# Index scores of two heads side by side, and accumulators emptied every 2.5 counting rounds instead of 2.8

## The reference, cut to what matters

```python
rel = jax.nn.relu(jnp.einsum('bqhd,bsd->bqhs', qi, k_idx))
score = jnp.einsum('bqh,bqhs->bqs', wi, rel).astype(jnp.float32)
score = jnp.where(key_pos[None, None, :] <= tq[None, :, None], score, -jnp.inf)
_, idx = lax.top_k(score, k_sel)
```

## Time and profile before

| | us |
|---|---|
| median of 3 runs | 4440.09 |
| lowest and highest | 4439.41, 4443.5 |
| the profiled execution | 4443.01 |
| its span in the trace | 4441.0 |
| TensorE busy (share of the span) | 3583.1 (81%) |
| VectorE busy | 2140.6 (48%) |
| GpSimd busy | 1159.3 (26%) |
| ScalarE busy | 1107.1 (25%) |
| mean granted clock of TensorE | 0.896 |

### The profile page before, as it was taken

One profiled execution on the slowest core, in us unless ns is written; L12 is line 12 of the kernel. 1 busy time (PEld: TensorE's weight loads), 2 busy tenths in 40 slices (PEclk: granted clock), 3 DMA queues, 4 the chain that ended last, 5 costly groups with the idle time before them and its releaser, 6 DMA issues. The chain is left out here.

```text
span 4441.0 us, 49671 instructions
## 1 busy us (share of the span) xinstructions
PE 3583.1 (81%) x18450; PEld 2762.6 (62%) x18450; DVE 2140.6 (48%) x3709; ACT 1107.1 (25%) x1965; POOL 1159.3 (26%) x654
## 2 busy tenths in 40 slices
PE   6787677657767677779999996689989778997978
PEld 4356555446666566568888785466756567665657
DVE  3579388774444424335555556503335450333552
ACT  2344133321112111110000001213335320333540
POOL 2013122212222344345444341231110233211112
PEclk7779889868888789889999998799989989998999
DMA  2001000000001111112221220210000121100011
GB/s 96 24 19 38 15 3 3 1 7 1 0 0 66 38 48 33 37 49 93 83 80 66 90 90 10 77 39 23 17 13 3 67 72 44 29 20 7 9 58 62
DMA packets 227900, 169.74 MB, mean 38 GB/s; under 512 B 42232, under 2 KB 214976, under 8 KB 226976
## 3 DMA queue, kind: packets, MB, share of 16 engines
q1 hardware_dynamic: 225152, 166.83, 12.0%
q10 hardware_dynamic: 2592, 0.81, 0.1%
HBM read 150.69 MB, written 16.92 MB: 38 GB/s over the span
## 5 line engine op out<-in xcount | busy, mean ns | idle before, releaser
L1434 DVE TENSOR_TENSOR I-12785S<-I-12785S,c_causal 128x256 f32<-128x256 f32 x64 | 27.7, 432 | 462.9 <-PE I-12785S L1372 462.9
L747 DVE TENSOR_TENSOR I-9738act_f<-I-9737act_g,I-9744p_u 128x1024 f32<-128x1024 f32 x22 | 26.9, 1222 | 321.9 <-PE I-9744p_u L259 167.3
L864 DVE SCALAR_TENSOR_TENSOR y_T<-y_T 128x1024 f32<-128x1024 f32 x48 | 131.9, 2786 | 0.0
L737 ACT ACTIVATE I-9737act_g<-I-9743p_g 128x1024 f32<-128x1024 f32 x22 | 22.6, 1029 | 419.5 <-PE I-9743p_g L259 419.5
L255 PE MATMUL I-9743p_g<-hf_hi,I-9719w_hi 128*128 128x512 f32 x352 | 109.5, 392 | 5.2 <-POOL hf_lo L473 5.2
L763 DVE TENSOR_TENSOR x_T<-x_T,I-9746p_d 128x512 f32<-128x512 f32 x176 | 112.5, 678 | 0.7 <-PE I-9746p_d L728 0.6
L763 DVE TENSOR_TENSOR x_T<-x_T,I-9745p_d 128x512 f32<-128x512 f32 x176 | 112.4, 677 | 0.4 <-PE I-9745p_d L728 0.4
L257 PE MATMUL I-9743p_g<-hf_lo,I-9719w_hi 128*128 128x512 f32 x352 | 109.0, 391 | 0.0
L259 PE MATMUL I-9743p_g<-hf_hi,I-9721w_lo 128*128 128x512 f32 x352 | 108.8, 390 | 0.0
L255 PE MATMUL I-9744p_u<-hf_hi,I-9720w_hi 128*128 128x512 f32 x352 | 108.4, 389 | 0.0
L257 PE MATMUL I-9744p_u<-hf_lo,I-9720w_hi 128*128 128x512 f32 x352 | 108.4, 389 | 0.0
(11 more groups left out here) (1035 smaller groups left out, 10457.1 us busy)
## 6 DMA issues: line engine op xcount, KB each, us to landing
y_T<-in_w_ada SPq DMA_DIRECT2D x48, 512.0 KB, 6.8
saved_x<-x_T SPq DMA_DIRECT2D x3, 4096.0 KB, 13.7
x_T<-saved_x SPq DMA_DIRECT2D x3, 4096.0 KB, 15.6
I-9717w_raw<-in_w_gate SPq DMA_DIRECT2D x22, 512.0 KB, 3.8
I-9718w_raw<-in_w_up SPq DMA_DIRECT2D x22, 512.0 KB, 4.1
I-12773w_raw<-in_w_in SPq DMA_DIRECT2D x16, 512.0 KB, 3.9
I-12774w_raw<-in_w_in SPq DMA_DIRECT2D x14, 512.0 KB, 3.9
I-9731d_raw<-in_w_down SPq DMA_DIRECT2D x11, 512.0 KB, 4.8
```

Of the source, the lines that this page charges most:

```text
L747: nc.vector.tensor_tensor(act_f[:, :], act_g[:, :], flat(p_u), ALU.mult).then_inc(product, 1)
L864: self.nc.vector.scalar_tensor_tensor(out=self.raw[s], in0=self.raw[s], scalar=1.0, in1=self.c_row, op0=ALU.mult, op1=ALU.mult, accum_out= ...
L1434: self.nc.vector.tensor_tensor(diag, diag, tiled(self.mask, 2), ALU.add).then_inc(self.masked, 1)
```

## The change

The units become (pair, tile, part of at most 512 columns), 40 of them: ten parts per pair, six of 512 columns, two of 384, one of 256 and one of 128. Each unit has both heads: two matmuls, on partitions 0 to 63 and 64 to 127, into the two banks of one score buffer; one Relu over both banks; and two weighings. VectorE does the weighing of a unit's second head one unit late, so that the first head of unit u comes, then the second head of unit u - 1. `project(2)` and `project(3)` stand in the middle of pairs 0 and 1. The conditions for writing a score or Relu buffer again are as before, counted anew. In counting, the rule for the rounds after which a `keep` runs is changed from `(r + 1) * 5 >= (done + 2) * 14` to `(r + 1) * 4 >= done * 10 + 8`.

```diff
-    units = [(n, h, t) for n in range(PAIRS) for h in range(2) for t in tiles]
+    parts = [(t, at, min((t + 1) * P - at, BANK)) for t in tiles for at in range(0, (t + 1) * P, BANK)]
+    units = [(n, t, at, w) for n in range(PAIRS) for t, at, w in parts]
...
-        relu = [v_T[:, s, :] for s in range(4)]
+        relu = [v_T[:, s, :].rearrange("p (h n) -> p h n", h=2) for s in range(4)]
...
-                for u, (n, h, t) in enumerate(units):
-                    if h == 1 and t == tiles[0] and n + 2 < PAIRS:
+                for u, (n, t, at, w) in enumerate(units):
+                    if u % len(parts) == len(parts) // 2 and n + 2 < PAIRS:
                         project(n + 2)
                     pe.wait_ge(q_ready, n + 1)
                     wait(pe, relu_done, u - 1)
-                    rows = slice(h * IDX_DIM, (h + 1) * IDX_DIM)
-                    score_columns(nc, S[u % 2], qi[n][rows, t * P:(t + 1) * P], key_T[rows, :], (t + 1) * P).then_inc(scores_ready, 1)
+                    for h in range(2):
+                        rows = slice(h * IDX_DIM, (h + 1) * IDX_DIM)
+                        last = nc.tensor.matmul(S[u % 2][:, h, 0:w], qi[n][rows, t * P:(t + 1) * P], key_T[rows, at:at + w], start=True, stop=True)
+                        last.then_inc(scores_ready, 1)
...
-                for u, (n, h, t) in enumerate(units):
-                    if h == 0 and t == tiles[0]:
+                for u, (n, t, at, w) in enumerate(units):
+                    if u % len(parts) == 0:
                         for m in ((0, 1) if n == 0 else (n + 1,) if n + 1 < PAIRS else ()):
                             act.wait_ge(q_used, m + 1)
                             nc.scalar.activation(qi[m], flat(acc[m % 2]), ACT.Copy).then_inc(q_ready, 1)
-                    w = (t + 1) * P
-                    act.wait_ge(scores_ready, u + 1)
-                    wait(act, weighed, u - 3)
-                    nc.scalar.activation(relu[u % 4][:, 0:w], flat(S[u % 2])[:, 0:w], ACT.Relu).then_inc(relu_done, 1)
-                act.wait_ge(weighed, len(units))
+                    act.wait_ge(scores_ready, 2 * (u + 1))
+                    wait(act, weighed, 2 * u - 5)
+                    nc.scalar.activation(relu[u % 4][:, :, 0:w], S[u % 2][:, :, 0:w], ACT.Relu).then_inc(relu_done, 1)
+                act.wait_ge(weighed, 2 * len(units))
...
-                    if done < NB and (r + 1) * 5 >= (done + 2) * 14:
+                    if done < NB and (r + 1) * 4 >= done * 10 + 8:
                         keep(done)
                         done += 1
...
-                for u, (n, h, t) in enumerate(units):
-                    w = (t + 1) * P
-                    dve.wait_ge(relu_done, u + 1)
-                    wait(dve, weighed, u - NS + 1)
-                    v.scalar_tensor_tensor(out=scores(t), in0=relu[u % 4][:, 0:w], scalar=head_w[:, t, 2 * n + h:2 * n + h + 1], in1=scores(t),
+
+                def weigh(u, h, after):
+                    n, t, at, w = units[u]
+                    into = scores(t)[:, at:at + w]
+                    wait(dve, weighed, after)
+                    v.scalar_tensor_tensor(out=into, in0=relu[u % 4][:, h, 0:w], scalar=head_w[:, t, 2 * n + h:2 * n + h + 1], in1=into,
                                            op0=ALU.mult, op1=ALU.add).then_inc(weighed, 1)
-                dve.wait_ge(weighed, len(units))
+
+                for u in range(len(units) + 1):
+                    if u < len(units):
+                        dve.wait_ge(relu_done, u + 1)
+                        weigh(u, 0, 2 * (u - len(parts)) + 3)
+                    if u > 0:
+                        weigh(u - 1, 1, max(1, 2 * (u - 1)))
+                dve.wait_ge(weighed, 2 * len(units))
```

## The result

The changed kernel takes 4382.5 us (median of 4 runs, 4382.0 to 4387.64) against 4441.8 for the kernel before (4 runs beside it, 4439.41 to 4451.33): 59.3 us less, a ratio of 0.9865 with a 95% interval of 0.9848 to 0.9882. The forecast was 4387, range 4375 to 4404. The profiled execution took 4382.19 us, its span is 4380.2.

What follows compares the result with a forecast made beforehand. Taken as bounds in turn: TensorE in scoring, VectorE in counting, TensorE in the tail. Scoring -35.6, extra splits +3.9 and tail -21.8 gave -53.5 us, from the median 4440.1 to 4387 us, range 4375 to 4404.

Steps and rivals of the forecast that it cites:

- Heads side by side: Scoring: two heads' matmuls overlap on TensorE, a pair costing 7.0 us, or 14.1 at 1.2 GHz, instead of 28.7.
- rival (e): Scoring: heads don't overlap, TensorE stays at 28.7 us a pair and only the tail gains, 4422 us; chance 0.04.
- 52.4 us of weighings: Scoring: VectorE's weighings for 8 heads, 6.56 us per head, priced from undisturbed durations in the earlier trace.
- Rival (d): Scoring: every weighing pays a hand-off of up to 0.2 us, its partner only just written, 4403 us; chance 0.04.
- project(2) 1.4 and project(3) 0: Scoring: VectorE's uncovered wait for project(2) is 1.4 us; project(3) finds a longer lead and costs nothing.
- The clock, 1.0: Scoring: an allowance of 1.0 us in all for falls of TensorE's granted clock.
- rival (b): The clock stays low through scoring and project(3) is uncovered, +8.5 us, 4395 us; chance 0.10.
- The split in scoring, 2.0: Scoring: POOL's weight-block split beside one 512-column weighing adds 2.0 us, 2.772 instead of 0.751.
- Two more splits at 1.95: Before ScalarE's last Sign: 15 splits instead of 13, at 1.95 us each, add 3.9 us.
- The rule of the shared port: VectorE beside GpSimd splits: full blocking would cost 4.3 us a split, 7.0 us more in sum; the forecast used partial blocking.
- rival (c): Each split blocks VectorE for its whole length, 4394 us; chance 0.06.
- The tail, -21.8: Behind the selection: two blocks are left instead of four, 2 x 10.88 us, 21.8 us less.

Runs made afterwards that it cites:

- e3: Changed kernel with both heads' score matmuls on array rows 0 to 63, so that they cannot run side by side: 4420.67 us.
- e9: Changed kernel with 14 of 16 GpSimd weight splits touching 8 columns instead of 1024, later blocks using stale weights: 4352.08 us.
- e11: On top of e6, each half of a split issued as four GpSimd instructions of 256 columns instead of one of 1024: 4357.69 us.
- e6: Changed kernel with keep 12 before the selection's first Sign and keep 13 behind its second: 4370.83 us.
- e4: Changed kernel with the second head's weighing directly behind the first's of the same unit, instead of one unit late: 4389.71 us.
- e8: On top of e6, project(2) and project(3) each cut into six pieces of two matmuls, one between each two units: 4373.28 us.
- e5: Changed kernel with a keep after every second counting round: 4375.89 us.
- e10: Changed kernel, unchanged, run once more with a profile: 4379.06 us.

## Why the prediction was right

**The bounds** were read rightly: TensorE, VectorE, TensorE. e3 shows the first, e9 and e11 the second, e6 the last.

**The total: right, in part by luck.** The stage gained 54.0 us for a forecast of 53.5 because -3.1 and -0.8 stood against +3.4. The median of 4382.5 lies 4.5 below 4387; in the profiled executions the untouched stages behind took 6.8 us less, and they vary by that much on their own.

**Heads side by side: right.** e3 is the proof; rival (e) falls.

**52.4 us of weighings: too high.** 80 of them took 49.0, with the split's cost already in it. The durations of the earlier trace rows were those of weighings in the old order; one instruction put between two that touch the same columns lets the next begin earlier (4.5 of the 5.4 us by which 52.4 + 2.0 was too high; e4 against the change). I had costed this order at 0 to 0.2 a weighing as a loss; it is a gain. Rival (d) has the wrong sign.

**project(2) 1.4 and project(3) 0: wrong, 2.17 and 2.16.** This follows from the term before. I had weighings of 52.4 / 40 = 1.31 us a unit against a loop of TensorE and ScalarE of 1.15, so that the lead would grow. At 49.0 / 40 = 1.23, the split among it, it hardly does, and both projects find VectorE with about 0.8 us in hand (2.96 - 2.17). The loop's 1.15 is my estimate and was not measured. With slower weighings the second wait fell to 0.93 (e4); cutting the work into pieces changed nothing (e8).

**The clock, 1.0: nothing.** It was 1.00 throughout scoring; rival (b) falls. I had read the earlier trace rows as a clock that fell with TensorE busy all the time. It stayed down with TensorE busy; it fell behind pauses of 0.94 and 0.20 us.

**The split in scoring, 2.0: about 2.5.** The weighing of 512 columns at 189 to 193 us took 2829 ns, as in the earlier trace rows, and that of 256 before it 920 instead of 470. So 52.4 + 2.0 + 1.4 + 0.5 + 1.0 became 49.0 + 4.7, and scoring ended at 221.2, not 224.3.

**Two more splits at 1.95: +3.9 was +7.3.** This is the step that failed worst. There were two more, 14 instead of 12 between mask add and last Sign. But the price from eight splits of the earlier trace rows is no constant: 30 free rounds are 114 us, so 28 us went in counting after and 21 before, on twelve and ten splits. The one ahead of counting added 3.9 (L1969, 1852 ns, and L1971, 2630 ns), and one split fewer beside the selection gave 3.5 back. The price hangs on where a round ends within a split, and every shift redraws it: e4 paid 6.5 us for a change in scoring.

**The rule of the shared port.** I wrote that the trace shows blocking, but not all of it, and gave rival (c) 0.06. The Trainium skill (SBUF — State Buffer, two separate sides) calls the port an exclusive lock held for a whole instruction, taken by a VectorE instruction with two SBUF inputs or in a two-port mode. The runs agree with it: the two-input L1978 and L1981 and the weighings stand until GpSimd's instruction ends, the counting reduces never do, and shorter GpSimd instructions shorten the stand (e11). The one-input L1971 and e11's L1993 stand too; whether they run in a two-port mode no row shows. My mistake was to apply the rule to the engine instead of to the instructions that it names; its price as I had worked it out, 4.3 a split, is still too high for counting, where a split cost 0.85 to 3.3 us.

**The tail, -21.8: -22.6**, two blocks as forecast. **Keep doesn't wait: right**. No keep of the changed kernel waits in counting; e5 (every two rounds) and e9 (rounds without splits) show where it begins to.

**Later stages keep their lengths:** as far as can be told; they vary by 10 us by themselves.

## What to carry to other kernels

Before an instruction's cost beside another engine is taken as a mean, look which instructions grow: here two of 6 columns bore all that counting lost, and cutting the other engine's instructions into quarters won 13 us of it. A forecast of a stage that comes out within a microsecond can be made of terms that miss by 3; check it term by term at the stage's own marks. And before calling an interruption of the faster engine free, ask how much faster it is per step: a lead of some per cent is gone as soon as the slower one turns out cheaper than costed.

## What the runs showed of the hardware

- A two-input VectorE instruction of 6 columns (0.17 us) took up to 2.25 us beside GpSimd's 1024-column subtraction and up to 0.76 beside 256-column instructions, and ended within 0.03 us of it; 896-column counting reduces kept 1142 ns. A one-input TENSOR_SCALAR was held too: 384 columns took 2.63 us instead of 0.42 (L1971 of the changed kernel), 6 columns 2.38 us in e10 and 0.67 in e11.
- Two 64-row matmuls of 512 columns on different row halves: 1.02 to 1.13 us for four records, 1.88 on one half. With one half in use the clock stayed at 0.50 with TensorE busy 33.65 of 34 us, and had fallen there behind short pauses; with both it stayed at 1.00 through longer ones (e3 and before against the change). Why the pauses cost the clock in one kernel and not in the other, these runs don't show.
- Putting an independent weighing between two dependent ones saved 0.11 us for each of the 40 dependent ones (4.5 us in sum, e4 against the change).
